# Attention scores of two layers: from plain f32 products to three products of rounded halves and rests

## The chip, the cores and the metric

The kernel runs on one core of one Trainium2 chip. The metric is the device time in microseconds (us) of one execution. TensorE (PE in the profile) multiplies, VectorE (DVE) and ScalarE (ACT) work element by element, GpSimd (POOL) prepares the weights, SyncE (SP) issues the weight loads.

## The reference, cut to what matters

A first block (attention, convolution, memory attention, a feed-forward net) is followed by two equal layers, `hybrid_layer`. The change touches the attention of these two. With 512 tokens, 8 heads of 64 and h = rmsnorm(x):

```
q_a, k_a, v_a, f_a, q_b, kv_b, g_b, gate_a, gate_b = split(h @ w_in)
# fox: 8 heads, causal, with a forget bias c
s = q_a . k_a * 64**-0.5 + c_i - c_j ; p = softmax(s) ; o_a = p @ v_a
# nsa: 8 query heads over 2 key heads, three branches
q   = partial_rope(q_b) ; ks, kw = partial_rope(ks), partial_rope(kw)
kc  = partial_rope(compress_blocks(kc))          # 31 compressed keys
s_c = q . kc * scale   (keys that end before i)  -> o_c
s_s = q . ks * scale   (chosen blocks: all 8)    -> o_s
s_w = q . kw * scale   (window of 512: all)      -> o_w
o_n = g0 * o_c + g1 * o_s + g2 * o_w
x   = x + (sigmoid(gate_a) * (o_a @ w_o_fox) + sigmoid(gate_b) * (o_n @ w_o_nsa)) @ w_out
```

All arrays are float32. With 512 tokens the chosen blocks are all blocks and the window reaches all keys, so both branches are plain causal attention.

## The kernel before, in words

**Matmuls in two precisions.** Every projection is one "tile": 128 output features by 512 tokens, eight chunks of 128 input features, each multiplied three times (lines 497 to 499): weights and activations are each split into a rounded half (`_hi`, type f32r) and a rest (`_lo`), and hi·hi, hi·lo and lo·hi are summed in PSUM. These are f32r matmuls. POOL splits each 128x1024 weight block (lines 442 and 445). The scores of the attention, lines 622 and 776, use the plain f32 type instead.

**The input phase of a layer** (layer 0: about 635 to 778 us, layer 1: about 1418 to 1562 us) runs through 27 jobs, `jobs = ph["in"]`: `gate, kz0, cmp0, kz1, cmp1, kz2, kz3`, then four times a `w1` (half-blocks of the compression weights) with four tiles: `qr0..qr3`, `kr0, kr1, v4, v5`, `v0..v3`, `cp0..cp3`. `kz` are the keys `ka` and `cp` the queries `qa` of fox; `qr` and `kr` are queries and keys of nsa, which need the rotary step. All engines walk the same list with an own loop; PE multiplies job i and then does `finish(i - 1)`; DVE and ACT do in step i what belongs to job i, i-1 or i-2. Each engine takes its instructions in the order of the program and waits at semaphores.

**The rotary step** of a tile i: ACT copies the tile out of PSUM as `rope_hi` (1262), DVE makes `rope_lo` (1711), PE multiplies both by a permutation into the one bank `ps[5]` (592 and 593, in `finish(i)`, which runs after tile i+1), and DVE in its step i+2 forms cosine part `t1` (1698), sine part (1700) and their sum `qb` or `ksw` (1703, 1705), with which it raises `roped`. The next rotation needs `ps[5]` free:

```
def rotate_split(n, slot):
    pe.wait_ge(roped, n - len(ROPE))
    nc.tensor.matmul(ps[5][:, :], rot_r[:, :], rope_hi[:, slot, :], start=True, stop=False)
```

**Attention.** A unit is one head by one block t of 128 queries; its scores are 128x(128(t+1)). Units go in groups of four: two heads, which lie in rows 0 to 63 and 64 to 127 of q and k, for blocks 0 and 3 or blocks 1 and 2. So a group has a pair of units of 128 and a pair of 512 columns, or of 256 and 384. A layer has 8 groups of fox and 16 of nsa. `scores` computes q·k (622; for fox a bf16 product with the forget bias goes first, 608), DVE adds the mask and takes the minimum (1435), ACT exponentiates (1053), DVE scales (1446), PE transposes (632), ACT copies back (1065), PE multiplies with the values (669, 672). In the nsa part a `gate` tile is multiplied in each group step. In the fox part four compressed scores (773 and 776) of 62 columns for four pairs of heads are done, into bank 3. The fox scores start while the last tile, `cp3`, is half done; bank order decides which unit needs which tile taken from PSUM: in layer 0 unit 2 uses the bank of `cp3`, in layer 1 bank 3, that of the compressed scores, held `cp3`.

Of the kernel before, what the change touches and what calls it, by code (L numbers as in the profile page):

```python
# [68 lines left out]
def build(nc, xT, memT, positions, wstream, params, fconst, bconst, lncount, trig2, out):  # L69
# [4 lines left out]
    with ctx:  # L74
# [69 lines left out]
        cmp_t = at("cmp_t", [2, S], f32, R + 66 * KIB)  # L144
        cmp_g = at("cmp_g", [2, 16, 64], f32, R + 70 * KIB)
# [3 lines left out]
        rot_r = at("rot_r", [P], f32r, R + 64 * KIB)  # L149
# [6 lines left out]
        yn_hi = at("yn_hi", [4, S], f32r, R + 52 * KIB)  # L156
        yn_lo = at("yn_lo", [4, S], f32r, R + 60 * KIB)
# [21 lines left out]
        bc = at("bc", [5 * P + 4 * 248 + 8 * P], bf16, Q)  # L179
        Q += (5 * P + 4 * 248 + 8 * P) * 2  # L180
# [33 lines left out]
        rope_split, rot_rounded = sem("rope_split"), sem("rot_rounded")  # L214
        rs_kept, rs_applied, rope_in, gated = sem("rs_kept"), sem("rs_applied"), sem("rope_in"), sem("gated")
# [32 lines left out]
                 "gg": "act", "add": "dve", "fg": "dve", "fu": "dve", "cp": "dve", "kz": "act",  # L248
# [229 lines left out]
        def _(pe):  # L478
# [116 lines left out]
            def scores(i, u0, freed, n=2):  # L595
# [13 lines left out]
                for u in range(i, i + n):  # L609
# [3 lines left out]
                    if kind == "b1":  # L613
                        q_, k_ = q1[r, h // 2, t * P:(t + 1) * P], k1[r, h // 2, :]
                    elif kind == "mem":
                        q_, k_ = qm[r, h // 2, t * P:(t + 1) * P], km[r, h // 2, :]
                    elif kind == "fox":
                        q_, k_ = qa[r, h // 2, t * P:(t + 1) * P], ka[r, h // 2, 0:w]
                    else:
                        q_ = qb[r, h % 4, t * P:(t + 1) * P]  # L620
                        k_ = ksw[r, 0 if kind == "sel" else 1, 0:w]
                    mm = nc.tensor.matmul(s_bank(u)[:, 0:w], q_, k_, start=kind != "fox", stop=True)  # L622
                    mm.then_inc(scored, 1)
# [142 lines left out]
            def compressed_scores(u0, t):  # L766
# [6 lines left out]
                nc.tensor.matmul(ps[3][:, 0:8 * NCMP], identb, cmask[:, t, :], start=True, stop=False)  # L773
                for pair in range(4):
                    both = ps[3][:, 0:8 * NCMP].rearrange("p (g s n) -> p g s n", g=2, s=4)[:, :, pair, :]
                    mm = nc.tensor.matmul(both, qb[:, pair, t * P:(t + 1) * P], kc[:, :, :], start=False, stop=pair == 3)
# [214 lines left out]
        def _(act):  # L991
# [83 lines left out]
            def attend(u0, un, gate_tiles):  # L1075
                for g in range(9):
# [31 lines left out]
            def compressed_exp(u0, t):  # L1108
# [4 lines left out]
                A(cprob[:, :, 0:NCMP], crow[:, 0:8 * NCMP].rearrange("p (h n) -> p h n", h=8), ACT.Exp,  # L1113
# [123 lines left out]
            for l in range(LAYERS):  # L1237
# [4 lines left out]
                for i in range(len(jobs) + 1):  # L1242
                    if i < len(jobs):
                        t = jobs[i]
                        kind, idx, _, _, bank = tiles[t][:5]
                        if kind in ("qr", "kr"):
                            act.wait_ge(blocks_done, filled(t))
                        elif kind not in ("cp", "w1"):
# [740 lines left out]
```

## Time and profile before

| | |
|---|---|
| median of 3 runs | 2212.59 us (2212.02 to 2216.07) |
| span of the profiled execution | 2210.5 us |
| busy PE / PEld / DVE / ACT / POOL | 99% / 78% / 53% / 28% / 68% |
| instructions | 29691 |
| HBM read | 191.85 MB, 88 GB/s over the span |

The profile gives the profiled execution's span only; the median of the runs is 2.1 us above it. PE is the matmul part of TensorE, PEld its loads of the stationary operand, which run beside the matmuls. A record's length holds the way through the array too, so the pace of matmuls is read from start to start. A f32 matmul leaves two PE records (two passes), an f32r matmul one.

### The profile page before, as it was taken

How to read it: one execution, taken by the hardware profiler on the slowest of the kernel's cores; microseconds unless marked ns; L12 is line 12 of the kernel's file. 1: busy time of each engine (PE TensorE's matmuls, PEld its weight loads, DVE VectorE, ACT ScalarE, POOL GpSimd, SP SyncE). 2: the span in 40 equal slices, each digit the busy share in tenths (PEclk: the TensorE clock that was granted, in tenths of full speed). 3: DMA queues.
4: the chain of work that ended last, by engine and by line, in shares of the span. 5: the costliest groups of instructions: out<-in, count | busy, mean ns of one | idle time of the engine just before them, and what ended most of it. 6: DMA issues, size and time to landing. Idle time of an engine off the chain costs nothing.

```text
span 2210.5 us, 29691 instructions
## 1 busy us (share of the span) xinstructions
PE 2184.6 (99%) x10906; PEld 1731.1 (78%) x10907; DVE 1176.8 (53%) x1950; ACT 608.8 (28%) x1439; POOL 1495.6 (68%) x679
## 2 busy tenths in 40 slices
PE   9999999999999999999999999999999999999998
PEld 6876788888887767778888888877677788888886
DVE  8769667774455285557640243562755477411422
ACT  5238322221011165531220121111555412200210
POOL 7660687778876614449887888766334398887884
PEclk9999999999999999999999999999999999999999
DMA  5320233333333312113333333333111132333332
GB/s 194 113 77 1 69 96 101 97 96 102 107 95 126 115 29 58 49 58 101 90 104 97 95 95 96 95 115 115 58 48 49 58 95 86 105 95 95 96 100 71
DMA packets 54921, 195.81 MB, mean 89 GB/s; under 512 B 7313, under 2 KB 7313, under 8 KB 54545
## 3 DMA queue, kind: packets, MB, share of 16 engines
q1 hardware_dynamic: 52496, 187.85, 28.3%
q10 hardware_dynamic: 2304, 6.26, 0.8%
q8 instruction: 88, 1.44, 0.3%
q14 instruction: 33, 0.26, 0.0%
HBM read 191.85 MB, written 2.10 MB: 88 GB/s over the span
## 4 chain that ended last, share of the span: by engine, by line
PE 92%; DVE 5%; ACT 1%; issue 1%; DMA 0%; POOL 0%; SPq 0%; DVEq 0%
PE bank L497 26%; PE bank L499 26%; PE bank L498 26%; PE bank L622 3%; PE bank L632 3%; PE bank L669 1%; DVE t L1333 1%; PE bank L651 1%; PE bank L672 1%; DVE prow L1446 1%; PE bank L510 1%; PE bank L579 1%; DVE bank L1435 1%; ACT prow L1053 1%; DMA w_raw<-wstream 0%
## 5 line engine op out<-in xcount | busy, mean ns | idle before, releaser
L442 POOL TENSOR_TENSOR w_hi<-w_raw,zero 128x1024 fp32r<-128x1024 f32 x336 | 651.5, 1939 | 662.9 <-PE bank L499 651.9
L445 POOL TENSOR_TENSOR w_lo<-w_raw,w_hi 128x1024 fp32r<-128x1024 f32 x336 | 845.2, 2515 | 26.4
L497 PE MATMUL bank<-hn_hi,w_hi 128*128 128x512 f32 x1632 | 646.8, 396 | 3.9 <-POOL w_lo L445 2.6
L499 PE MATMUL bank<-hn_hi,w_lo 128*128 128x512 f32 x1632 | 636.5, 390 | 0.0
L498 PE MATMUL bank<-hn_lo,w_hi 128*128 128x512 f32 x1632 | 636.1, 390 | 0.0
L497 PEld LDWEIGHTS bank<-hn_hi,w_hi 128*128 128x128 f32 x1632 | 306.9, 188 | 73.6 <-issue 5.2
L499 PEld LDWEIGHTS bank<-hn_hi,w_lo 128*128 128x128 f32 x1632 | 306.6, 188 | 65.4
L498 PEld LDWEIGHTS bank<-hn_lo,w_hi 128*128 128x128 f32 x1632 | 307.0, 188 | 62.5 <-issue 1.4
L497 PE MATMUL bank<-hid_hi,w_hi 128*128 128x512 f32 x688 | 267.7, 389 | 0.0
L499 PE MATMUL bank<-hid_hi,w_lo 128*128 128x512 f32 x688 | 267.6, 389 | 0.0
L498 PE MATMUL bank<-hid_lo,w_hi 128*128 128x512 f32 x688 | 267.6, 389 | 0.0
L1506 DVE TENSOR_TENSOR x<-bank,x 128x512 f32<-128x512 f32 x64 | 44.2, 691 | 372.8 <-PE bank L499 372.8
L1306 ACT ACTIVATE sq<-tmp 128x512 f32<-128x512 f32 x64 | 40.4, 632 | 431.4 <-DVE tmp L1824 431.4
L499 PEld LDWEIGHTS bank<-hid_hi,w_lo 128*128 128x128 f32 x688 | 129.1, 188 | 27.0
L498 PEld LDWEIGHTS bank<-hid_lo,w_hi 128*128 128x128 f32 x688 | 129.2, 188 | 26.9
L497 PEld LDWEIGHTS bank<-hid_hi,w_hi 128*128 128x128 f32 x688 | 129.1, 188 | 26.6
L1824 DVE SCALAR_TENSOR_TENSOR tmp<-bank,rs 128x512 f32<-128x512 f32 x64 | 44.1, 692 | 185.0 <-PE bank L499 185.0
L1065 ACT ACTIVATE pT<-bank 128x256 f32<-128x256 f32 (+2 forms) x240 | 98.1, 453 | 140.4 <-PE bank L632 139.6
L1828 DVE TENSOR_TENSOR hid_lo<-sq,hid_hi 128x512 fp32r<-128x512 f32 x64 | 123.2, 1929 | 1.5 <-ACT hid_hi L1308 1.5
L1435 DVE CUSTOM_DVE_ANT_0 bank<-bank,bc 128x128 f32<-128x128 f32 (+1 forms) x192 | 89.5, 520 | 63.5 <-PE bank L622 63.5
L632 PEld LDWEIGHTS bank<-fc,prow 128*128 128x128 f32 x640 | 68.4, 141 | 57.3 <-issue 29.9
L1039 ACT ACTIVATE hn_hi<-x,par 128x512 fp32r<-128x512 f32 x40 | 29.0, 724 | 273.3 <-DVE x L1506 273.3
(304 smaller groups left out, 2646.9 us busy)
## 6 DMA issues: line engine op xcount, KB each, us to landing
w_raw<-wstream SPq DMA_DIRECT2D x352, 512.0 KB, 3.6
x<-xT SPq DMA_DIRECT2D x4, 512.0 KB, 7.6
out<-yout ACTq DMA_DIRECT2D x8, 256.0 KB, 2.2
mem_x<-memT SPq DMA_DIRECT2D x1, 1024.0 KB, 12.2
lnc<-lncount ACTq DMA_DIRECT2D x1, 1024.0 KB, 5.9
cs<-trig ACTq DMA_DIRECT2D x2, 512.0 KB, 4.4
par<-params ACTq DMA_DIRECT2D x1, 696.0 KB, 5.2
bc<-bconst ACTq DMA_DIRECT2D x1, 664.0 KB, 7.1
```

Source lines behind the costliest of these rows:

```text
L442: nc.gpsimd.tensor_tensor(w_hi[:, slot, :], w_raw[:, slot, :], zeros, ALU.add).then_inc(w_rounded, 1)
L445: nc.gpsimd.tensor_tensor(w_lo[:, slot, :], w_raw[:, slot, :], w_hi[:, slot, :].bitcast(f32), ALU.subtract).then_inc(w_split, 1)
L497: nc.tensor.matmul(ps[bank][:, 0:cols_], wh, a_h, start=c == 0, stop=False)
L498: nc.tensor.matmul(ps[bank][:, 0:cols_], wh, a_l, start=False, stop=False)
L499: mm = nc.tensor.matmul(ps[bank][:, 0:cols_], wl, a_h, start=False, stop=c == chunks - 1)
L622: mm = nc.tensor.matmul(s_bank(u)[:, 0:w], q_, k_, start=kind != "fox", stop=True)
L632: mm = nc.tensor.transpose(ps[4 + u % 2][:, c * P:(c + 1) * P], prow[:, u % 4, c * P:(c + 1) * P], ident)
L1065: A(turned(u)[:, u % 4, 0:width(u)], ps[4 + u % 2][:, 0:width(u)], ACT.Copy).then_inc(p_kept, 1)
L1435: V.tensor_tensor_reduce(out=s_bank(u)[:, 0:w], in0=s_bank(u)[:, 0:w], in1=causal[:, S - w:S], scale=1.0, scalar=3e38, op0=ALU.add, op1=AL ...
L1506: V.tensor_tensor(x[:, m, :], ps[tiles[t][4]][:, :], x[:, m, :], ALU.add).then_inc(dve_took, 1)
L1824: V.scalar_tensor_tensor(out=tmp[:, n % 3, :], in0=ps[tiles[up[i]][4]][:, :], scalar=0.0, in1=rs[:, :], op0=ALU.max, op1=ALU.mult).then_in ...
L1828: V.tensor_tensor(hid_lo[:, i - 1, :], sq[:, (n - 1) % 2, :], hid_hi[:, i - 1, :].bitcast(f32), ALU.subtract).then_inc(ff_lo, 1)
```

## The change

It replaces each f32 product q·k of fox and nsa by three f32r products, q_hi·k_hi, q_hi·k_lo, q_lo·k_hi, summed in PSUM; the two units of a pair alternate. The compressed scores are done likewise, on 32 instead of 31 columns per key head (the mask covers the 32nd). For that, `qa`, `ka`, `qb`, `ksw` and `kc` become pairs `_hi` and `_lo`: ACT writes `_hi`, DVE subtracts it from the value in PSUM to get `_lo`. The rotated sum stays in `ps[5]` until both are taken. The buffers are laid out anew (`qb_lo` 54, `ksw_lo` 64, `qa_hi` 68, `qa_lo` 76 KiB into the region; `yn_hi` and `yn_lo` now lie where `qb` does; `lf`, `fgs`, `z32`, `s8`, `rot_r`, `cmp_t`, `cmp_g` moved). ACT does the exponentials of the first two fox rows before it takes `cp3`.

```diff
@@ scores(): after the bias products of fox
-                    elif kind == "fox":
-                        q_, k_ = qa[r, h // 2, t * P:(t + 1) * P], ka[r, h // 2, 0:w]
...
-                    mm = nc.tensor.matmul(s_bank(u)[:, 0:w], q_, k_, start=kind != "fox", stop=True)
-                    mm.then_inc(scored, 1)
+                for i2 in range(i, i + n, 2):
+                    for part in range(3):
+                        for u in (i2, i2 + 1):
...
+                            if kind == "fox":
+                                q_, k_ = (qa_hi, qa_hi, qa_lo)[part], (ka_hi, ka_lo, ka_hi)[part]
...
+                            mm = nc.tensor.matmul(s_bank(u)[:, 0:w], q_, k_, start=kind != "fox" and part == 0,
+                                                  stop=part == 2)
@@ compressed_scores()
-                    mm = nc.tensor.matmul(both, qb[:, pair, t * P:(t + 1) * P], kc[:, :, :], start=False, stop=pair == 3)
+                    for part in range(3):
+                        q_, k_ = (qb_hi, qb_hi, qb_lo)[part], (kc_hi, kc_lo, kc_hi)[part]
+                        mm = nc.tensor.matmul(both, q_[:, pair, t * P:(t + 1) * P], k_[:, :, :], start=False,
+                                              stop=pair == 3 and part == 2)
@@ ACT, input phase, step i
+                    if 0 <= i - 2 < len(jobs) and tiles[jobs[i - 2]][0] in ("qr", "kr"):
...
+                        act.wait_ge(rope_full, 6 * l + idx_of_rope(jobs[i - 2]) + 1)
+                        A((qb_hi if kind == "qr" else ksw_hi)[:, idx, :], ps[5][:, :], ACT.Copy).then_inc(rope_rounded, 1)
...
+                        elif kind == "cp":
+                            if i == len(jobs) - 1:
+                                exp_row(FIRST["fox", l])
+                                exp_row(FIRST["fox", l] + 1)
+                            act.wait_ge(cp_scaled, 4 * l + idx + 1)
+                            A(qa_hi[:, idx, :], src[:, :], ACT.Copy).then_inc(cp_rounded, 1)
@@ DVE, input phase, step i: (a) rotary of job i-2, (b) rope_lo or scale of job i, then
-                            V.tensor_tensor(qb[:, idx, :], ps[5][:, :], t1[:, :], ALU.add).then_inc(roped, 1)
+                        V.tensor_tensor(ps[5][:, :], ps[5][:, :], t1[:, :], ALU.add).then_inc(rope_full, 1)
...
+                    if 0 <= i - 2 < len(jobs) and tiles[jobs[i - 2]][0] in ("qr", "kr"):
...
+                        dve.wait_ge(rope_rounded, 6 * l + idx_of_rope(jobs[i - 2]) + 1)
+                        V.tensor_tensor(lo[:, idx, :], ps[5][:, :], hi[:, idx, :].bitcast(f32),
+                                        ALU.subtract).then_inc(roped, 1)
+                    if 0 <= i - 1 < len(jobs) and tiles[jobs[i - 1]][0] in ("kz", "cp"):
...
+                        V.tensor_tensor(lo[:, idx, :], ps[bank][:, :], hi[:, idx, :].bitcast(f32),
+                                        ALU.subtract).then_inc(dve_took, 1)
```

DVE in the input phase of layer 0, around the tiles `qr1` to `qr3`, before (`cs` is the sine and cosine table, `t` is `t1`):

```order
L1711 SCALAR_TENSOR_TENSOR rope_lo<-bank,rope_hi 128x512 [waits rope_in]
L1698 SCALAR_TENSOR_TENSOR t_124<-bank,cs_110 128x512 [waits roped,rotated,trig_scaled,fg_parts]
L1700 TENSOR_TENSOR bank<-bank,cs_110 128x512
L1703 TENSOR_TENSOR qb<-bank,t_124 128x512 [waits dve_took,dve_chain]
L1711 SCALAR_TENSOR_TENSOR rope_lo<-bank,rope_hi 128x512 [waits rope_in]
L1698 SCALAR_TENSOR_TENSOR t_124<-bank,cs_110 128x512 [waits roped,rotated,trig_scaled,fg_parts]
```

and the same place of the changed kernel:

```order
L1744 SCALAR_TENSOR_TENSOR rope_lo<-bank,rope_hi 128x512 [waits rope_in]
L1735 SCALAR_TENSOR_TENSOR t_130<-bank,cs_116 128x512 [waits roped,rotated,trig_scaled,fg_parts]
L1737 TENSOR_TENSOR bank<-bank,cs_116 128x512
L1739 TENSOR_TENSOR bank<-bank,t_130 128x512 [waits dve_took,dve_chain]
L1744 SCALAR_TENSOR_TENSOR rope_lo<-bank,rope_hi 128x512 [waits rope_in]
L1754 TENSOR_TENSOR qb_lo<-bank,qb_hi 128x512 [waits rope_rounded]
L1735 SCALAR_TENSOR_TENSOR t_130<-bank,cs_116 128x512 [waits roped,rotated,trig_scaled,fg_parts]
```

What frees `ps[5]` (and raises `roped`) was the fourth row; now it is the sixth, and the `rope_lo` of a tile two jobs later stands ahead of it.

DVE a few tiles on, around job `v4`, where `scale` (L1349 before, L1386 now) multiplies the new tile by the norm factor; before:

```order
L1698 SCALAR_TENSOR_TENSOR t_124<-bank,cs_110 128x512 [waits roped,rotated,trig_scaled,fg_parts]
L1700 TENSOR_TENSOR bank<-bank,cs_110 128x512
L1705 TENSOR_TENSOR ksw<-bank,t_124 128x512 [waits dve_took,dve_chain]
L1349 TENSOR_TENSOR bank<-bank,rs 128x512 [waits blocks_done]
L1698 SCALAR_TENSOR_TENSOR t_124<-bank,cs_110 128x512 [waits roped,rotated,trig_scaled,fg_parts]
```

and now:

```order
L1735 SCALAR_TENSOR_TENSOR t_130<-bank,cs_116 128x512 [waits roped,rotated,trig_scaled,fg_parts]
L1737 TENSOR_TENSOR bank<-bank,cs_116 128x512
L1739 TENSOR_TENSOR bank<-bank,t_130 128x512 [waits dve_took,dve_chain]
L1386 TENSOR_TENSOR bank<-bank,rs 128x512 [waits blocks_done]
L1754 TENSOR_TENSOR ksw_lo<-bank,ksw_hi 128x512 [waits rope_rounded]
L1735 SCALAR_TENSOR_TENSOR t_130<-bank,cs_116 128x512 [waits roped,rotated,trig_scaled,fg_parts]
```

Here the scaling of `v4` stands ahead of the subtraction that frees `ps[5]`.

PE in the fox part of layer 0, the scores of a pair with 384 columns; before (L622 is one instruction for each unit, with two passes; the numbers are the banks):

```order
L608 MATMUL bank0<-c3_96,bc_133 128x384
L608 MATMUL bank1<-c3_96,bc_133 128x384
L622 MATMUL bank0<-ka_87,qa_86 128x384
L622 MATMUL bank1<-ka_87,qa_86 128x384
L632 MATMUL bank4<-fc_132,prow_126 128x128 x4
```

and now (the bias products, L616, and the pair of 256 columns stand ahead of it):

```order
L642 MATMUL bank0<-ka_hi_87,qa_hi_88 128x384
L642 MATMUL bank1<-ka_hi_87,qa_hi_88 128x384
L642 MATMUL bank0<-ka_lo_86,qa_hi_88 128x384
L642 MATMUL bank1<-ka_lo_86,qa_hi_88 128x384
L642 MATMUL bank0<-ka_hi_87,qa_lo_89 128x384
L642 MATMUL bank1<-ka_hi_87,qa_lo_89 128x384
```

Two instructions with four passes became six with one pass each.

## Rows read from the trace of the kernel before

**Rows 1.** The page: busy us (share of the span) xinstructions, by engine
```profile
PE 2184.6 (99%) x10906; PEld 1731.1 (78%) x10907; DVE 1176.8 (53%) x1950; ACT 608.8 (28%) x1439; POOL 1495.6 (68%) x679
```
**Rows 2.** Waits, whole span: engine tile <- released by: us, times, longest
```profile
POOL w_hi L442 <- PE bank L499: 651.9, 273, 73.3
```
**Rows 3.** Busy in stretches (fox, nsa of layer 0): us, engines (x), PEclk, DMA share, GB/s
```profile
779.00:821.00 42.00, 39.25 (x306) 25.30 (x308) 37.85 (x143) 28.83 (x97) 3.76 (x2) 1.00 0.09 26
821.00:970.00 149.00, 149.00 (x900) 109.30 (x901) 84.84 (x256) 83.08 (x269) 63.81 (x30) 1.00 0.18 54
```
**Rows 4.** Timeline, PE, two groups of nsa: start, us, engine, line, what
```profile
868.68 1.35 PE L622 MATMUL bank<-ksw,qb 64*128 64x128 f32 x8
869.96 1.09 PE L632 MATMUL bank<-fc,prow 128*128 128x128 f32 x8
...
878.06 1.35 PE L622 MATMUL bank<-ksw,qb 64*128 64x256 f32 x8
879.34 1.09 PE L632 MATMUL bank<-fc,prow 128*128 128x128 f32 x8
```
**Rows 5.** Timeline, PE, a pair of 512 columns and compressed scores, layer 0
```profile
779.76 1.13 PE L622 MATMUL bank<-ka,qa 64*128 64x512 f32 x4
780.82 0.28 PE L773 MATMUL bank<-bc 128*128 128x248 bf16 x1
780.94 1.00 PE L776 MATMUL bank<-kc,qb 128*128 128x62 f32 x8
781.78 0.38 PE L608 MATMUL bank<-c,bc 96*128 96x256 bf16 x2
```
**Rows 6.** Timeline, PE, f32r matmuls of 256 columns in the first block
```profile
79.19 0.28 PE L497 MATMUL bank<-mn_hi,w_hi 128*128 128x256 f32 x1
79.31 0.28 PE L498 MATMUL bank<-mn_lo,w_hi 128*128 128x256 f32 x1
```
**Rows 7.** Timeline of all engines, rotary steps of layer 0
```profile
691.22 0.39 PE L592 MATMUL bank<-rope_hi,rot_r 128*128 128x512 f32 x1
691.42 0.60 ACT L1262 ACTIVATE rope_hi<-bank 128x512 fp32r<-128x512 f32 x1 [6.58 <-PE bank L499]
691.45 0.39 PE L593 MATMUL bank<-rope_lo,rot_r 128*128 128x512 f32 x1
692.05 0.69 DVE L1711 SCALAR_TENSOR_TENSOR rope_lo<-bank,rope_hi 128x512 fp32r<-128x512 f32 x1 [2.79 <-ACT rope_hi L1262]
692.66 0.68 DVE L1698 SCALAR_TENSOR_TENSOR t<-bank,cs 128x512 f32<-128x512 f32 x1
...
697.11 0.39 PE L592 MATMUL bank<-rope_hi,rot_r 128*128 128x512 f32 x1
...
701.57 0.39 PE L592 MATMUL bank<-rope_hi,rot_r 128*128 128x512 f32 x1
...
703.65 0.69 DVE L1703 TENSOR_TENSOR qb<-bank,t 128x512 f32<-128x512 f32 x1
```
**Rows 8.** Timeline, the rotation after tile v4, layer 0
```profile
717.85 0.39 PE L592 MATMUL bank<-rope_hi,rot_r 128*128 128x512 f32 x1
...
718.05 0.70 DVE L1349 TENSOR_TENSOR bank<-bank,rs 128x512 f32<-128x512 f32 x1 [3.86 <-PE bank L499]
```
**Rows 9.** Timeline, after the last tile cp3: layer 0, then layer 1
```profile
778.48 0.69 DVE L1729 SCALAR_TENSOR_TENSOR qa<-bank,rs 128x512 f32<-128x512 f32 x1 [0.39 <-PE bank L499]
779.23 0.61 PE L608 MATMUL bank<-c,bc 96*128 96x512 bf16 x2 [0.57 <-DVE qa L1729]
...
1562.39 0.69 DVE L1729 SCALAR_TENSOR_TENSOR qa<-bank,rs 128x512 f32<-128x512 f32 x1 [0.47 <-PE bank L499]
...
1564.00 0.28 PE L773 MATMUL bank<-bc 128*128 128x248 bf16 x1
```
**Rows 10.** The longest idle time of PE: timeline, and the stretch behind it
```profile
9.19 0.50 PE L497 MATMUL bank<-hn_hi,w_hi 128*128 128x512 f32 x1 [2.62 <-POOL w_lo L445]
...
12.00:20.00 8.00, 7.89 (x30) 6.05 (x29) 7.33 (x12) 6.86 (x13) 7.12 (x4) 0.87 1.01 407
```

More of the change, by code:

```diff
@@ L148, in build @@
         rope_lo = at("rope_lo", [2, S], f32r, R + 20 * KIB)
-        rot_r = at("rot_r", [P], f32r, R + 64 * KIB)
+        rot_r = at("rot_r", [P], f32r, R + 80 * KIB + 512)
         cs2 = at("cs2", [2, S], f32, R + 82 * KIB)
@@ L1241, in _ @@
                 jobs = ph["in"]
-                for i in range(len(jobs) + 1):
+                for i in range(len(jobs) + 2):
+                    if 0 <= i - 2 < len(jobs) and tiles[jobs[i - 2]][0] in ("qr", "kr"):
+                        kind, idx = tiles[jobs[i - 2]][:2]
+                        act.wait_ge(rope_full, 6 * l + idx_of_rope(jobs[i - 2]) + 1)
+                        A((qb_hi if kind == "qr" else ksw_hi)[:, idx, :], ps[5][:, :], ACT.Copy).then_inc(rope_rounded, 1)
                     if i < len(jobs):
@@ L1247, in _ @@
                             act.wait_ge(blocks_done, filled(t))
+                            if kind == "qr" and idx == 0:
+                                act.wait_ge(cmp_full, 2 * (l + 1))
                         elif kind not in ("cp", "w1"):
@@ L1270, in _ @@
                             ins.then_inc(act_took, 1)
-                    if i >= 1:
+                    if 1 <= i <= len(jobs):
                         t = jobs[i - 1]
@@ L1792, in _ @@
                             rows = slice(64 * g, 64 * g + 64)
-                            ins = V.tensor_tensor(kc[rows, g, :], tmp[rows, 0, sl], tmp[rows, 1, sl], ALU.add)
-                        ins.then_inc(cmp_kept, 1)
-                link(V.memset(cprob[:, :, NCMP:32], 0.0))
+                            link(V.tensor_tensor(kc[rows, g, 0:NCMP], tmp[rows, 0, sl], tmp[rows, 1, sl], ALU.add))
+                        link(V.tensor_copy(kc_hi[:, :, :], kc[:, :, :]))
+                        V.tensor_tensor(kc_lo[:, :, :], kc[:, :, :], kc_hi[:, :, :].bitcast(f32),
+                                        ALU.subtract).then_inc(cmp_kept, 1)
                 attend(FIRST["fox", l], FIRST["nsa", l], ph["gates"])
@@ L1949, in _constants @@
     q = np.arange(S).reshape(TT, P).T
-    cmask = np.where(end[None, None, None, :] <= q[:, :, None, None], f(0), f(BIG))
-    cmask = np.broadcast_to(cmask, (P, TT, 8, NCMP)).reshape(P, -1)
+    last = np.append(end, S)
+    cmask = np.where(last[None, None, None, :] <= q[:, :, None, None], f(0), f(BIG))
+    cmask = np.broadcast_to(cmask, (P, TT, 8, 32)).reshape(P, -1)
     sel = np.zeros((P, 8, P), f)
```

102 lines of the change are left out of this document (62 added, 40 removed).

## The prediction

> **What bounds the kernel now.** I read the page first: PE is busy for 2184.6 of 2210.5 us [rows 1]. Then who waits: POOL, which prepares the weights, waits 651.9 us for PE to free a block [rows 2], so neither weights nor DMA hold PE back. Then the stretches that the change touches. In the nsa part PE is busy for all of its 149 us; in the fox part for 39.25 of 42 us, with DVE at 37.85 beside it, so there the two share the bound [rows 3]. Hence the rule of the whole sum: a microsecond added to or taken from PE's stream counts in full, except in fox, and so does each moment in which PE, which takes matmuls in order, stands before a semaphore. The last point is seen in the trace: after cp3 PE stood idle 0.57 us until DVE had taken the tile [rows 9].
>
> **The scores, per pass.** A pair of 512 columns takes from 779.76 to 780.82, 1.06 us, for four records: both row halves run at once, so that is two passes. f32r matmuls of 512 columns start 0.23 us apart (691.22, 691.45) [rows 7]. A nsa group takes 1.28 us in both kinds (868.68 to 869.96, 878.06 to 879.34) [rows 4, 5]. The group of blocks 0 and 3 is a pair of 128 and a pair of 512 columns: 1.28 - 1.06 = 0.22 us for the two passes of 128 columns, 0.11 each. A pass in proportion to its columns is then 0.43 for 512, 0.215 for 256 and 0.325 for 384, and 1.06 - 2 x 0.43 = 0.20 us is left for the load ahead and the drain behind, which the switch between 128 and 64 rows lays bare once in each group.
>
> Now three f32r passes each. 512 columns: 0.23. 256 columns: 0.12 (79.19, 79.31) [rows 6]. 384: 0.175, midway. 128 columns have no row; what bounds them from below is the load of the stationary operand, which eight records of 62 columns show at 0.84/8 = 0.105 us, and I take 0.11 [rows 5]. From above: as two f32 passes, 0.22; I come to that as a rival. The kind (0, 3) goes from 2 x 0.11 + 2 x 0.43 = 1.08 to 3 x 0.11 + 3 x 0.23 = 1.02: 0.06 less. The kind (1, 2) goes from 2 x 0.215 + 2 x 0.325 = 1.08 to 3 x 0.12 + 3 x 0.175 = 0.885: 0.195 less. All this assumes that f32r pairs on 64 rows run at once as the f32 pairs do.
>
> The Trainium skill, in "TensorE: Matmul & The Clock Gate", section "LDWEIGHTS (loading the stationary operand)", says that this load takes a time set by the columns, at 1.2 per ns, whatever the rows: 107 ns. The row agrees with it (105 ns), and it speaks against this change, because a half-height operand is loaded three times where two loads were: by the page's figure the narrow pair would go from 0.22 to an estimated 0.32 us and win nothing.
>
> **nsa**: 16 groups in a layer, 8 of each kind: 8 x 0.255 = 2.04 us less; two layers: **-4.1**, in full, because PE is the bound there.
>
> **fox**: 8 groups: 4 x 0.255 = 1.0 us less in a layer. The compressed scores go from 8 records to 12 of 64 columns, at 0.11 us each: 0.44 more, four times: 1.75 more. If PE alone counted, +0.75 in a layer; DVE's share hides some. The ends are -1.0 (all added PE time hidden) and +1.75; I take +0.35, two layers: **+0.7**. DVE's own work here grows by 8 columns in a few instructions, nothing.
>
> **The rotary steps.** This is the largest term. `ps[5]`, which the next rotation overwrites, was free after the sum (L1703). Now it stays taken until ACT has copied it and DVE has subtracted, and DVE's subtraction stands behind `rope_lo` of the tile two jobs later. That in turn waits for ACT's copy of a tile that PE has only just finished. But PE's next instruction, right behind that same tile, is the rotation that needs `ps[5]`. So what was long done becomes a wait that can't be shorter than this chain, read from the tile qr2 [rows 7]: PE reaches the rotation at 691.22; ACT copies from 691.42 to 692.02; DVE makes `rope_lo` from 692.05; its next instruction starts 0.61 later, at 692.66, and would be the subtraction: 0.69, to 693.35 (sources in PSUM and SBUF as for L1703). PE reacts 0.06 later, as after cp3 (778.48 + 0.69 to 779.23) [rows 9], and then loads with nothing to overlap, half of the 0.20 above: 693.5. That is 2.3 us instead of none. The copy of the rotated tile by ACT itself is hidden, since the rotation before it is 5.9 us old.
>
> Which rotations: that of qr1 (behind qr2), and that of qr2 (behind qr3). The one of qr3 comes after half a w1 and half a tile, 4.46 us after qr2's (697.11, 701.57). Its chain has no new tile in it: rotation to end of sum 703.65 + 0.69 - 701.57 = 2.77, ACT 0.05 + 0.60, DVE 0.03 + 0.69, PE 0.06: 4.20. It fits with 0.26 to spare; nothing lost, 0.3 if I am wrong. kr0's waits for qr3's `ps[5]`, whose subtraction runs during kr1: nothing. kr1's (behind v4) waits for kr0's subtraction, which stands behind the scaling of v4: 718.05 + 0.61 + 0.69 + 0.06 + 0.10 = 719.5 against 717.85 [rows 8]: 1.65. The others are not followed by a rotation. A layer: 2 x 2.3 + 1.65 = 6.25, two layers **+12.5**. Ends: each link could be 0.1 shorter or longer: 11 to 14.
>
> **The start of fox.** cp3 is now scaled in PSUM, copied by ACT, subtracted by DVE. From the start of the scaling: 0.69 + 0.05 + 0.60 + 0.03 + 0.69 + 0.06 = 2.12. Layer 0, unit 2 needs the bank: 778.48 + 2.12 = 780.6 instead of 779.23: 1.4. Layer 1, only the compressed scores do: 1562.39 + 2.12 = 1564.5 instead of 1564.0: 0.5 [rows 9]. Together **+1.9**. The moved exponentials were done long before.
>
> **At nothing**: the other copies and subtractions, 4 kz, 3 cp and the narrow ones of `kc` in a layer. DVE is busy for 53% and ACT for 28% [rows 1], and those banks are used again two or more tiles (5.4 us each) later; each would cost its 0.7 us if that cover were gone. The new layout of buffers moves no instruction and I find no new wait in it. POOL and SP have the same instructions.
>
> **Sum**: -4.1 + 0.7 + 12.5 + 1.9 = +11.0 us on the span of 2210.5: 2221.5. The median of the runs lies 2.1 above the span, so 2223.6.
>
> **Rivals.**
> 1. *Narrow f32r matmuls are no faster than f32 ones.* Against it: 256 columns run at 0.12 [rows 6]; for it: no row below 256. A product of 128 then costs 0.22 instead of 0.11 in 24 pairs of 128 (12 in a layer), 24 x 0.33 = +7.9, and 96 compressed products 0.1 more each, +9.6, part of both hidden in fox. About +12: 2236.
> 2. *f32r pairs don't run on the two row halves at once.* For it: no row shows such a pair. Against it: f32 pairs and the 64-column products do. Each group's passes double: +1.02 and +0.885 in 48 groups = +46, less what fox hides: 2262.
> 3. *The stalls let the clock fall.* PE's longest idle time now is 2.62 us, at the start, and the stretch behind it had a granted clock of 0.87 [rows 10], which is a mix of the two levels, 1.2 and 2.4 GHz. It cost 8 x 0.13 = 1.0 us or more. Four stalls of 2.3 us at 1.0 to 1.7 each: +4 to +7: 2229. Against it: each new stall has more than 5 us of dense matmuls on both sides, and the start had little ahead of it.
> 4. *The other side: PE isn't held at the rotation.* If the next tile's matmuls, whose bank and weights are ready, went past the waiting rotation, the 12.5 would vanish: -4.1 + 0.7 + 1.9 = -1.5: 2211.1, not slower. It decides from the point where 11 of the 12.5 are hidden. Against it: at 779.23 PE stood idle for 0.57 us, and the next gate tile or transposes behind it did not go ahead [rows 9].
>
> **How the numbers follow.** Forecast 0.68, rival 1 0.08, rival 2 0.06, rival 3 0.12, rival 4 0.06. The forecast's own range, from the ends of its terms (scores -3 to -5, fox -1 to +2, rotary 11 to 14, start 1 to 2.5), is 2219 to 2228. The range for 8 in 10 goes from there up over rival 3 and nearly to rival 1: 2217 to 2234. A measurement of this kernel can tell 0.2%, 4.4 us, from no change. Rival 4 is "within", with some of its own spread below -0.2%, and a little of the forecast's lower tail falls within: slower 0.88, same 0.08, faster 0.04.
>
> **What would show it.** In the trace after: idle time of PE before `rope_hi` x `rot_r` (L600) of 2.2 us for qr1 and qr2 and 1.5 for kr1, in both layers, released by DVE's subtraction (L1754), none for qr0, qr3 and kr0; score groups of nsa of about 1.2 and 1.1 us instead of 1.28; f32r records of 64 rows starting in pairs some ns apart; twelve compressed records in 1.3 us; granted clock 1.00 throughout. Idle time before L600 below 1 us refutes the largest term; score groups above 1.3 us refute the second.

## The result, and the profile after

The changed kernel takes 2233.16 us (median of 4 runs, 2230.57 to 2234.36), the kernel before 2212.60 (4 runs beside it, 2212.02 to 2216.07): a ratio of 1.0088, 95% interval 1.0077 to 1.01, so 20.6 us slower. 2223.6 was forecast, with a range to 2234: the sign and the range hold, the most likely value was 9.6 us too low. The profiled run is the slowest of the four, 2234.36 us; its span is 2232.6 against 2210.5, so 22.1 us are to be explained.

The page after, beside [rows 1]: PE has 224 more matmuls (four in each of the 48 groups of pairs, four in each of the eight compressed products) and 9.2 us more busy time, less than half of the 22.1.

```profile
PE 2193.8 (98%) x11130; PEld 1749.8 (78%) x11131; DVE 1195.5 (54%) x1980; ACT 622.1 (28%) x1459; POOL 1495.4 (67%) x679
```

To find the place, I took the start of the same instruction in both traces and subtracted: the offset. The step is what the offset grew by since the row above (ahead of the first row it is +0.4, that of qr0's rotation, 685.15 before and 685.58 after). "Clock at 0.5" counts the stretches with a granted clock of 0.5 since the row above, called falls from here on; those at the start and the end of the kernel are left out.

```
start (us) of                     before    after   offset   step   clock at 0.5
rotation qr1, layer 0             691.22   693.91    +2.70   +2.3
rotation qr2, layer 0             697.11   703.78    +6.67   +4.0    1 (694.5)
rotation qr3, layer 0             701.57   709.89    +8.33   +1.7    1 (704.7)
rotation kr1, layer 0             717.85   727.82    +9.97   +1.6
first fox bias, layer 0           774.78   784.86   +10.07   +0.1
first compressed scores, layer 0  780.82   792.12   +11.30   +1.2
first nsa scores, layer 0         820.84   834.71   +13.87   +2.6    1 (800.3)
first tile of the mix, layer 0   1020.73  1032.74   +12.01   -1.9
rotation kr1, layer 1            1501.77  1523.38   +21.61   +9.6    2 (1489.8, 1500.0)
first compressed scores, layer 1 1564.00  1586.23   +22.23   +0.6
first nsa scores, layer 1        1604.02  1628.01   +23.99   +1.8    1 (1588.8)
first tile of the mix, layer 1   1803.92  1826.04   +22.11   -1.9
```

The largest term of the prediction, the rotary steps, is where it was put. PE's waits in layer 0 from the rotary steps to fox (engine, tile and line it waited in, releaser: us, times, longest):

```profile
PE bank L600 <- DVE qb_lo L1754: 4.2, 2, 2.1
PE bank L616 <- DVE qa_lo L1761: 1.9, 1, 1.9
PE bank L600 <- DVE ksw_lo L1754: 1.5, 1, 1.5
```

And the chain at qr1's rotation, from the timeline of all engines (start, us, engine, line, what, idle time ahead):

```profile
691.42 0.39 PE L507 MATMUL bank<-hn_hi,w_lo 128*128 128x512 f32 x1
691.85 0.60 ACT L1299 ACTIVATE rope_hi<-bank 128x512 fp32r<-128x512 f32 x1 [1.52 <-PE bank L507]
...
692.48 0.69 DVE L1744 SCALAR_TENSOR_TENSOR rope_lo<-bank,rope_hi 128x512 fp32r<-128x512 f32 x1 [2.78 <-ACT rope_hi L1299]
693.09 0.68 DVE L1754 TENSOR_TENSOR qb_lo<-bank,qb_hi 128x512 fp32r<-128x512 f32 x1
...
693.91 0.47 PE L600 MATMUL bank<-rope_hi,rot_r 128*128 128x512 f32 x1 [2.10 <-DVE qb_lo L1754]
...
703.78 0.47 PE L600 MATMUL bank<-rope_hi,rot_r 128*128 128x512 f32 x1 [2.10 <-DVE qb_lo L1754]
...
727.82 0.47 PE L600 MATMUL bank<-rope_hi,rot_r 128*128 128x512 f32 x1 [1.47 <-DVE ksw_lo L1754]
```

PE ends the tile, ACT copies, DVE makes rope_lo, DVE subtracts and only then releases ps[5]. In [rows 7] and [rows 8] the same rotations stood without idle time. What the forecast did not have is in the next view, the stretches around these waits (us, busy of PE, PEld, DVE, ACT, POOL, granted clock, DMA share, GB/s):

```profile
691.40:694.50 3.10, 1.00 (x5) 0.53 (x4) 1.29 (x2) 0.60 (x1) 2.53 (x2) 1.00 0.27 107
694.50:697.90 3.40, 3.40 (x10) 2.63 (x9) 2.00 (x3) 0.60 (x1) 1.74 (x1) 0.50 0.01 2
697.90:704.70 6.80, 4.70 (x23) 3.30 (x23) 1.37 (x3) 0.60 (x1) 2.79 (x2) 1.00 0.00 0
704.70:708.10 3.40, 3.40 (x13) 2.09 (x10) 2.61 (x4) 0.60 (x1) 1.47 (x1) 0.50 0.23 46
```

Right behind each wait of 2.1 us the granted clock is 0.50, the lower of the two levels (1.2 GHz), and PE does 10 and 13 matmuls in a time in which it does 15 at full clock. That happens at all four waits of 2.1 us, and once more in each layer's fox part:

```profile
796.80:800.30 3.50, 2.27 (x18) 1.50 (x20) 3.28 (x15) 2.89 (x10) 0.00 (x0) 1.00 0.01 2
800.30:803.70 3.40, 3.40 (x18) 2.21 (x16) 2.74 (x12) 2.36 (x8) 0.00 (x0) 0.50 0.00 0
```

The scores. Timeline of PE, one nsa group of each kind, to be held against [rows 4]:

```profile
882.03 0.33 PE L642 MATMUL bank<-ksw_hi,qb_hi 64*128 64x128 f32 x2
882.19 0.28 PE L642 MATMUL bank<-ksw_lo,qb_hi 64*128 64x128 f32 x2
882.30 0.28 PE L642 MATMUL bank<-ksw_hi,qb_lo 64*128 64x128 f32 x2
882.42 0.45 PE L642 MATMUL bank<-ksw_hi,qb_hi 64*128 64x512 f32 x2
882.70 0.40 PE L642 MATMUL bank<-ksw_lo,qb_hi 64*128 64x512 f32 x2
882.93 0.41 PE L642 MATMUL bank<-ksw_hi,qb_lo 64*128 64x512 f32 x2
883.26 0.98 PE L654 MATMUL bank<-fc,prow 128*128 128x128 f32 x7
...
891.38 0.39 PE L642 MATMUL bank<-ksw_hi,qb_hi 64*128 64x256 f32 x2
...
892.45 1.09 PE L654 MATMUL bank<-fc,prow 128*128 128x128 f32 x8
```

Each row is a pair (x2) on the two row halves, and the next pass starts 0.11 us later at 128 columns and 0.23 at 512, behind the first pass of each 0.05 more: pairs run at once, and narrow f32r matmuls are fast. The groups take 1.23 (forecast 1.22) and 1.07 us (forecast 1.085). The start of fox in layer 0 and the compressed scores, against [rows 9] and [rows 5]:

```profile
790.69 0.60 PE L616 MATMUL bank<-c,bc 96*128 96x512 bf16 x2 [1.93 <-DVE qa_lo L1761]
791.23 0.49 PE L642 MATMUL bank<-ka_hi,qa_hi 64*128 64x512 f32 x2
...
792.16 0.28 PE L800 MATMUL bank<-kc_hi,qb_hi 128*128 128x64 f32 x1
792.27 0.28 PE L800 MATMUL bank<-kc_lo,qb_hi 128*128 128x64 f32 x1
...
793.39 0.28 PE L800 MATMUL bank<-kc_hi,qb_lo 128*128 128x64 f32 x1
793.51 0.40 PE L616 MATMUL bank<-c,bc 96*128 96x256 bf16 x2
```

Twelve records in 1.35 us, 0.11 each, where eight took 0.84.

### The profile page after: what moved, and what is told of

Same layout as the page of the kernel before. It is cut to its first block, busy times and chain, and to the rows that moved or that the text cites. A ratio compares the mean times of both kernels' runs of the same rounds, so it can differ in the third digit from the quotient of the medians.

```text
span 2232.6 us, 30187 instructions
## 1 busy us (share of the span) xinstructions
PE 2193.8 (98%) x11130; PEld 1749.8 (78%) x11131; DVE 1195.5 (54%) x1980; ACT 622.1 (28%) x1459; POOL 1495.4 (67%) x679
## 4 chain that ended last, share of the span: by engine, by line
PE 91%; DVE 5%; issue 1%; ACT 1%; DMA 0%; POOL 0%; SPq 0%; DVEq 0%
PE bank L505 26%; PE bank L507 26%; PE bank L506 26%; PE bank L654 3%; PE bank L642 2%; PE bank L691 1%; DVE t L1370 1%; PE bank L627 1%; PE bank L673 1%; PE bank L518 1%; PE bank L694 1%; DVE prow L1483 1%; PE bank L587 1%; DVE bank L1472 0%; PE bank L800 0%
```

## The experiments

Ten kernels were measured, in four runs each where no number is given; the kernel before took 2212.7 to 2213.0 (medians) beside them. One run of each was profiled, and what is said of waits and of falls is read from that one. "Offset" is, as above, against the trace of before.

**e1: the subtraction first.** In DVE's step the block at L1754 stands ahead of rope_lo:

```diff
+                    if 0 <= i - 2 < len(jobs) and tiles[jobs[i - 2]][0] in ("qr", "kr"):
+                        ...
+                        V.tensor_tensor(lo[:, idx, :], ps[5][:, :], hi[:, idx, :].bitcast(f32),
+                                        ALU.subtract).then_inc(roped, 1)
                     if i < len(jobs) and tiles[jobs[i]][0] in ("qr", "kr"):
                         ... rope_lo ...
                     if i < len(jobs) and jobs[i] in SCALED:
                         scale(jobs[i])
-                    (the same block)
```

> The changed kernel with one block moved: in DVE's step the subtraction that frees ps[5] stands ahead of rope_lo and of the scaling of the tile two jobs later. Theory A (the rotation of qr1, qr2 and kr1 waits because the subtraction stands behind rope_lo, and the clock falls because of that wait): PE's idle time before rope_hi x rot_r goes from 2.1, 2.1 and 1.5 us to none in both layers, 12.3 us less, and the four stretches with a granted clock of 0.5 behind qr1's and qr2's rotations go with them, 4 x 1.7 = 6.8 us less: 2233.2 - 12.3 - 6.8 = about 2214. Rival B (the clock falls there because of the work in the rotary steps, not of the wait): only the stalls go, about 2221. Rival C (the wait is really for ACT's copy or for rope_lo itself, whatever the order): 2233.

Measured: 2217.10 us (10 runs, 2215.86 to 2219.01). The rotations of qr1 and qr2 have the offset of the kernel's start, +0.3; 0.5 us more come before qr3's, with a wait of 0.35, and stay (L1744 is the moved subtraction, L1751 rope_lo):

```profile
690.24 0.69 DVE L1744 TENSOR_TENSOR qb_lo<-bank,qb_hi 128x512 fp32r<-128x512 f32 x1 [0.67 <-ACT qb_hi L1271]
...
691.53 0.39 PE L600 MATMUL bank<-rope_hi,rot_r 128*128 128x512 f32 x1
...
692.36 0.69 DVE L1751 SCALAR_TENSOR_TENSOR rope_lo<-bank,rope_hi 128x512 fp32r<-128x512 f32 x1 [1.43 <-ACT rope_hi L1299]
```

The subtraction now runs 1.3 us before PE gets to the rotation, under a tile's matmuls. All four falls in the rotary steps are gone too. A instead of B and C: 16 of the 20.6 us go with one moved block. It is 3 us above A's 2214, with its ratio at 1.0018 (1.0009 to 1.0028). Against A, the profiled execution has 0.5 us more before qr3's rotation in each layer, and the wait of 1.9 us for cp3's bank was followed by a longer fall than those that A left in place, 781.8 to 792.0. Layer 0's rotary steps, then that fall:

```profile
691.00:715.00 24.00, 23.65 (x110) 17.99 (x109) 12.44 (x19) 5.82 (x9) 16.39 (x8) 1.00 0.30 102
```

```profile
781.80:792.00 10.20, 10.20 (x46) 7.01 (x45) 5.87 (x21) 3.85 (x13) 2.00 (x1) 0.50 0.18 53
```

**e4: the kernel before, with the order alone changed.** The sum `V.tensor_tensor(qb, ps[5], t1)` (L1703) moved behind rope_lo and the scaling, and ACT's wait before `rope_hi` put on `rotated` instead of `roped`, as in the changed kernel; nothing is split, and all scores are plain f32.

> The kernel before with nothing but the order changed: DVE's sum that frees ps[5] stands behind rope_lo and the scaling of the tile two jobs later, as in the changed kernel; scores and everything else are plain f32 as before. Theory A (the order alone makes the stalls, the stalls make the clock fall): 2 x 6.2 = 12.3 us of stalls and four stretches at clock 0.5 for 6.8 us: 2212.6 + 19.1 = about 2231.7. Rival B (order gives the stalls but the fall of the clock needs the f32r copies or scores too): about 2225. Rival C (the stalls come from ACT's added copy in the chain rather than from the order): 2212.6, no change.

Measured: 2232.08 us (2229.03 to 2235.63), the time of the changed kernel and A's 2231.7. Its timeline:

```profile
692.45 0.69 DVE L1705 SCALAR_TENSOR_TENSOR rope_lo<-bank,rope_hi 128x512 fp32r<-128x512 f32 x1 [3.58 <-ACT rope_hi L1262]
693.06 0.68 DVE L1716 TENSOR_TENSOR qb<-bank,t 128x512 f32<-128x512 f32 x1
...
693.89 0.47 PE L592 MATMUL bank<-rope_hi,rot_r 128*128 128x512 f32 x1 [2.17 <-DVE qb L1716]
```

The same wait, 2.17 us, with no copy of the rotated tile by ACT. So the order makes the stall, and C falls, and B with it: the clock falls without the f32r copies and scores of the change. The profiled execution, the fastest (2229.03), has two of the four falls (703.0 and 1494.9): behind the same wait of 2.2 us the clock sometimes stays up. The four times, 2229.03, 2230.70, 2233.45 and 2235.63, go with mean clocks of 0.997, 0.997, 0.995 and 0.994.

**e2 and e8: PE kept busy in the wait.** Both leave every semaphore as it is and put bf16 matmuls into a spare bank ahead of the rotation:

```diff
                     if kind in ("qr", "kr"):
                         pe.wait_ge(rot_rounded, l + 1)
+                        if t in (jobs[9], jobs[10], jobs[14]):        # qr1, qr2, kr1
+                            stay_awake(9 if t != jobs[14] else 6)     # e8: 4, and none at kr1
```

> The changed kernel with bf16 matmuls of 512 columns into the spare bank put on PE just ahead of the rotations that wait (9 each ahead of qr1's and qr2's, 6 ahead of kr1's), so that PE works where it stood idle for 2.1 or 1.5 us; the wait for DVE's subtraction stays. Theory A (idle PE lets the clock fall): the rotations start as late as before, but the four stretches at clock 0.5 behind them go: 4 x 1.7 = 6.8 us less than the changed kernel's 2233.2, about 2226.5. Rival B (the falls have another cause than the idle PE): the falls stay, 2233. Rival D (the added matmuls last longer than the idle time): up to 2 us more than either, shown by no idle time left ahead of the rotation.

> The changed kernel with 4 instead of 9 bf16 matmuls of 512 columns put on PE ahead of the rotations of qr1 and qr2, and none ahead of kr1's: 0.9 of 2.1 us is filled and about 1.2 us of idle time is left. The stalls stay as long. Theory A (the clock falls behind a long idle time, and 1.2 us is not enough): the four stretches at 0.5 go in most executions, mean clock 0.996 to 0.997, about 2226.4 to 2229. Rival B (any idle time of over a microsecond amid dense work does it): the falls stay, clock 0.994 to 0.995, about 2232 to 2234.

Measured: e2 2229.01 us (2228.56 to 2230.76), e8 2229.03 (2228.19 to 2230.64). The rotations come as late as in the changed kernel (6.3 to 6.4 us have come together by kr1's rotation, in both kernels and layers), but no fall lies behind them. First e2, then e8, layer 0, where 1.23 us of idle time was left; for each, the timeline (it has eight of the nine matmuls of e2) and then the stretch:

```profile
691.99 1.89 PE L565 MATMUL bank<-bc 128*128 128x512 bf16 x8
694.03 0.47 PE L600 MATMUL bank<-rope_hi,rot_r 128*128 128x512 f32 x1
```

```profile
691.00:715.00 24.00, 23.64 (x107) 16.72 (x107) 10.55 (x16) 3.56 (x6) 12.85 (x6) 1.00 0.24 85
```

```profile
691.34 1.04 PE L565 MATMUL bank<-bc 128*128 128x512 bf16 x4
693.60 0.47 PE L600 MATMUL bank<-rope_hi,rot_r 128*128 128x512 f32 x1 [1.23 <-DVE qb_lo L1756]
```

```profile
691.00:706.00 15.00, 12.55 (x58) 8.34 (x57) 7.16 (x11) 2.40 (x4) 8.58 (x4) 1.00 0.13 44
```

So stall and clock are two costs with two cures. From qr1's to qr2's rotation the changed kernel takes 9.87 us and e2 8.26: 1.6 us is what one such fall costs. The medians come down by 4.1 us, not by 6.4. The changed kernel's 2233.2 does not stand for four falls in every run (its fastest took 2230.57), and more of the fox part ran at 0.5 here: in e2 a fall of 10.2 us (788.3 to 798.5), in e8 one of 6.8 (789.4) and one of 3.4, where the changed kernel has two of 3.4. e2 is 2.5 us above A's 2226.5, of which an estimate of 1.7 is that longer fall (3.4 us more at half the clock). In e8 the upper end of A's 2226.4 to 2229 holds, with its mean clocks of 0.996 and 0.997; its rival B falls.

**e3: the scores as one f32 product.** `for part in range(1)` with `q_.bitcast(f32), k_.bitcast(f32)`, in all three kinds of score.

> The changed kernel with each of the three-part scores (fox, nsa, compressed) as one f32 product of the two rounded halves; it leaves out the two products with the rests. All that ACT and DVE produce, all waits and the order are those of the changed kernel. It gives the price of the products alone. nsa: groups go back to 1.28 us, 2 x 1.74 = 3.5 us more. fox: compressed scores 12 records of 0.11 become 8, 1.75 less in all, pairs 2.0 more, partly hidden by DVE. Theory A (the clock falls in fox, at 800.3 and 1588.8, because the f32r scores give PE less work between its waits): both falls go, 3.4 us less: 2233.2 + 3.5 + 0.3 - 3.4 = about 2233.5. Rival B (they fall because of the idle time ahead of cp3's bank and cmask): they stay, about 2237. In both the stalls of the rotary steps and the four falls there stay.

Measured: 2234.23 us (2231.62 to 2236.82). The nsa part is back to before's length to 0.03 us, the stalls and the four falls stay, there is none in fox, and one more behind kr1's wait of 1.5 us (1523.8). So A rather than B, but on one profiled execution, and the four times, 2231.6 to 2236.8, reach from one to the other. In fox the three parts cost what is missing here: from the first compressed scores to the first nsa scores layer 0 takes 39.95 us, 40.02 in the kernel before, 42.59 in the changed one with one fall in it.

**e5: the banks too.** e1, and the cp tiles on banks 0 to 3 in both layers, with `first = (0, 1, 2, 7)` as the order of the score banks, so that unit 2 needs cp2's bank.

> The kernel of e1 (subtraction ahead of rope_lo) and the q tiles cp0 to cp3 on banks 0 to 3 in both layers, so that unit 2 of fox in layer 0 needs cp2's bank and no longer cp3's; only the compressed scores still wait for cp3, as in layer 1. In e1's trace PE stood idle for 1.9 us ahead of unit 2 in layer 0, and a stretch of 10.2 us with a granted clock of 0.5 lay there; from the start of fox to the first nsa score layer 0 lost 6.0 us and layer 1 1.55 us. Theory A (the wait for cp3's bank costs 1.2 us and is also what lets the clock fall): layer 0 becomes like layer 1, 4.4 less than e1's 2217.1: about 2212.7. Rival B (the clock falls in fox because three short f32r passes leave PE less work, wait or not): only 1 us less, about 2216, with a stretch at 0.5 still in layer 0's fox part.

Measured: 2213.33 us (10 runs, 2212.08 to 2215.71), ratio 1.000 (0.9991 to 1.0009): the changed computation at the time of the kernel before. The wait before unit 2 is gone, 0.57 us before the compressed scores is left. The ten times lie in three groups, near 2212.3, 2213.8 and 2215.6; the profiled one of the last group has a fall in each fox part (789.4 and 1574.4). The five fastest, 2212.08 to 2212.87, are A's 2212.7, and B is half right: falls in fox don't need cp3's wait. The fall in layer 0:

```profile
789.40:792.80 3.40, 3.40 (x18) 2.45 (x16) 2.89 (x12) 1.49 (x6) 0.00 (x0) 0.50 0.00 0
```

**e6 and e7: split from SBUF.** e6 leaves DVE's order and writes the sum to t1, so that ps[5] is free at once; e7 scales the cp tiles into `tmp` as well.

```diff
-                        V.tensor_tensor(ps[5][:, :], ps[5][:, :], t1[:, :], ALU.add).then_inc(rope_full, 1)
+                        V.tensor_tensor(t1[:, :], ps[5][:, :], t1[:, :], ALU.add).then_inc(rope_full, 1)
             def rotate_split(n, slot):
-                pe.wait_ge(roped, n - len(ROPE))
+                pe.wait_ge(rope_full, n - len(ROPE))
```

> The changed kernel, DVE's order as it is there, but the rotated sum is written to t1 in SBUF instead of back to ps[5]; ACT copies and DVE subtracts from t1, and PE's next rotation waits for the sum alone (rope_full). Theory A (the stalls come from ps[5] being held until the subtraction): PE's idle time before all six rotations of a layer is gone, the 0.5 before qr3's that e1 still had too, and no stretch at 0.5 behind them: 2233.2 - 12.3 - 6.8 = 2214.1, up to 2 more for a longer fall in fox as in e1. Rival B (the order of DVE's instructions delays rope_lo or the sum itself so that PE waits all the same): above 2217. ACT's copy and the subtraction may take another time from SBUF than from PSUM; nothing waits for them.

> The kernel of e6, and the scaled q tiles (cp) are written to tmp in SBUF as well, so that their banks are free from the scaling on as in the kernel before; ACT and DVE split them from there, and the fox scores wait for the finished pair of tiles by a semaphore. Theory A (all waits of the change were for PSUM held through the split): no idle time of PE beyond that of before in the rotary steps (12.3 us less than the changed kernel) and at the start of fox (1.2 and 0.5 less), none of the six stretches at 0.5. What is left of the change is nsa -1.74 in each layer, fox +0.9 to +1.0 in each, the start of the kernel +0.3: 2212.6 - 3.5 + 2.0 + 0.3 = about 2211.4, 0.05% less than before. Rival B (the clock falls in fox without the waits too, from its lighter f32r work): 1.7 to 5 us more, 2213 to 2216.

Measured: e6 2216.69 us (10 runs, 2213.95 to 2217.71), e7 2215.95 (11 runs, 2213.16 to 2220.03; ratio 1.0012, 1.0003 to 1.0021). The stalls of 2.1 and 1.5 us are gone in both, so A's cause holds (e6 is 0.6 us above A's upper end), but e7 misses A's 2211.4 and is no faster than e5. Its rival B, falls in fox without the waits, has the number (2213 to 2216), and e7's profile has such a fall at 789.6, e6's one at 1570.2. Two more things were priced wrong. Before qr3's rotation 0.51 us of waiting stays in each layer. It is now for the sum, which starts late because the subtraction ahead of it takes longer from SBUF. The subtractions of e7 by source (min/median/max ns), and those of one of them beside POOL:

```profile
L1762 DVE TENSOR_TENSOR qb_lo<-t,qb_hi x8: 692/1021/1318, 693.2 to 1493.5; 128x512 fp32r<-128x512 f32 x8
L1762 DVE TENSOR_TENSOR ksw_lo<-t,ksw_hi x4: 1878/1912/1947, 720.0 to 1512.3; 128x512 fp32r<-128x512 f32 x4
...
L1769 DVE TENSOR_TENSOR qa_lo<-tmp,qa_hi x8: 1058/1129/1167, 761.5 to 1566.7; 128x512 fp32r<-128x512 f32 x8
```

```profile
719.48 1.90 POOL L450 TENSOR_TENSOR w_hi<-w_raw,zero 128x1024 fp32r<-128x1024 f32 x1 [3.21 <-PE bank L507]
720.04 1.88 DVE L1762 TENSOR_TENSOR ksw_lo<-t,ksw_hi 128x512 fp32r<-128x512 f32 x1
...
721.45 2.73 POOL L453 TENSOR_TENSOR w_lo<-w_raw,w_hi 128x1024 fp32r<-128x1024 f32 x1
```

From PSUM the same subtraction took 0.69 us in all twelve cases of e1. The second: the fox part of layer 1 stays 1.73 us longer than before's although cp3's wait of 0.54 is gone, where e1 had 1.55 with it. So taking the wait away gained nothing there, and what counts is the scores' own work.

**e9 and e10: which scores cost it in fox.** e5, with the compressed scores alone as one f32 product of the rounded q, and with the fox pairs alone so.

> The kernel of e5 (no rotary stalls but 0.5 before qr3, no wait for cp3's bank before unit 2) with the compressed scores alone as one f32 product of the rounded q with the f32 key, 8 records instead of 12; it leaves out the products with the rest of q. It asks how much of fox's surplus the four added records of each of the four compressed products of a layer are. e5 takes 2212.2 in its executions without a fall of the clock, and a layer's fox part 45.32 + 1.55 in e1's layer 1. Theory A (the records count in full: 4 x 4 x 0.11 = 1.8 a layer): 2212.2 - 3.6 = 2208.6 at the lowest, median about 2209.5. Rival B (DVE and ACT set the end in fox, the records are hidden): no less than 2211.5. Between the two, each in part: 2210.

> The kernel of e5 with the fox pairs alone as one f32 product of the rounded halves; it leaves out their products with the rests. The compressed and nsa scores keep three parts. By the passes (1.0 us a layer saved by the three short f32r passes) PE has 2 x 1.0 us more to do in fox. Theory A (fox is bound by PE): 2212.2 + 2.0 = 2214.2 in executions without a fall of the clock. Rival B (fox is bound by DVE, pairs are hidden): 2212.2 or up to 0.5 less. On the clock: if the lighter three-part pairs are what lets it fall in fox, as e3's profile without a fall there suggests, all executions stay at 0.999 and the times lie within 1 us of each other, where e5's lay in three groups 1.7 apart; if not, the three groups stay.

Measured: e9 2209.58 us (10 runs, 2209.01 to 2211.20; ratio 0.9988, 0.9978 to 0.9997), e10 2212.96 (10 runs, 2212.68 to 2213.55). The fox part of layer 1 (first bias to first nsa scores) of before, e1, e9 and e10, one row each, none with a fall in it (e1 stands for e5, whose profile has a fall there; in this layer both have the same waits):

```profile
1558.70:1604.02 45.32, 42.78 (x325) 28.05 (x325) 40.04 (x150) 29.63 (x101) 7.11 (x4) 1.00 0.11 34
```

```profile
1564.31:1611.18 46.87, 43.83 (x373) 31.66 (x373) 40.46 (x150) 30.43 (x102) 7.04 (x4) 1.00 0.11 34
```

```profile
1557.48:1602.81 45.33, 42.11 (x357) 29.91 (x356) 40.51 (x150) 30.27 (x102) 7.09 (x4) 1.00 0.11 35
```

```profile
1559.56:1606.72 47.16, 44.48 (x342) 29.82 (x341) 40.96 (x150) 30.38 (x102) 7.19 (x4) 1.00 0.11 33
```

With eight compressed records instead of twelve the part is as long as before: of the four products' four added records each, 1.8 us at 0.11, 46.87 - 45.33 = 1.54 lie on the path (e9, A; its median is the 2209.5 that A gave). The pairs do the opposite: their three short passes leave PE 0.65 us less to do (44.48 - 43.83), of which 0.29 reach the end (47.16 - 46.87), between e10's A and B. On the clock: e10's ten times lie within 0.9 us, where e5's lay over 3.6. Over all twelve profiles, the four kernels with f32 pairs in fox (before, e3, e4, e10) have no fall in either layer's fox part; of the eight with three-part pairs, seven have at least one, and e9 none, though four of its ten times stand apart from the other six, 1 us above them. That points to the lighter pairs as what lets it fall there, and e3, which has the waits of the changed kernel, speaks against the waits as its cause. Five of the ten falls in fox begin 1.7 to 2.4 us behind a wait of PE of 1.2 us before a transpose, but six more such waits have none behind them. It isn't settled: the executions of the kernel before, with f32 pairs, lie between 2212.0 and 2216.1, some of them 1.7 or 3.4 us above the rest, and only one of them was profiled.

## Why the prediction was right, and where it was not

By its own terms, us on the span of the profiled executions; "measured" is taken from traces in which no fall lies in that part.

```
term                     forecast  measured  from
rotary stalls              +12.5     +12.7   e2: 6.33 and 6.36 to kr1's rotation
start of fox                +1.9      +1.8   after: 1.23 and 0.54
nsa scores                  -4.1      -3.7   after: -1.86 a layer
fox scores                  +0.7      +2.0   e1, layer 1: +1.00, twice
start of the kernel          0        +0.4   +0.1 to +0.9 from execution to execution
the rest: falls of clock     0        +8.9   6.4 rotary, 2.3 fox; a rival at +4 to +7
sum                        +11.0     +22.1
```

**The rotary steps** were right in place, size and chain: waits before qr1, qr2 and kr1, none before qr0, qr3, kr0, in both layers, and the rotations late by 2.3, 2.4 and 1.65 us (e2) where 2.3, 2.3 and 1.65 were worked out from the rows of before. e1 and e4 show the cause from both sides: the place of one DVE instruction behind another that needs a tile PE has just ended. Rival 4, that PE isn't held, fell.

**The nsa scores** were right by kind, 1.23 and 1.07 us. Rivals 1 and 2 fell with them: pairs of 128 columns pass in 0.11 us and both row halves run at once. The 0.20 us that was put down to one switch in each group came out right as a sum, but lies in three places of the first group's rows: 0.05 behind the first pass of 128, 0.05 behind the first of 512, 0.10 before the transposes.

**The fox scores** failed in one term, "DVE's share hides some". I took +0.35 a layer between ends of -1.0 and +1.75, as if DVE hid a part of what is added; it came to +1.0. e9 shows 1.54 of the added 1.8 on the path, and e10 that the pairs' saving, which I had set at 1.0 in full, brings 0.29 and takes 0.65 from PE's busy time. The row had it: PE is busy for 39.25 of 42 us [rows 3], so most of what is added to PE there must lengthen the part. Even PE alone, +0.75 by my own terms, was nearer than the value I chose.

**The clock** is the step that failed. The prediction had "granted clock 1.00 throughout" among its signs, and against rival 3, the falling clock, it wrote: "Against it: each new stall has more than 5 us of dense matmuls on both sides". With that it gave rival 3, 2229, a chance of 0.12, and it is what happened: 6.4 of the 8.9 us stand behind the four waits of 2.1 us, and e2 and e8 take them away with the stalls left in place. The price of 1.0 to 1.7 us for each holds (1.6), though only its lower end had a row. The one row on it [rows 10], 2.62 us of idle time with 0.87 behind it, was the nearest to a wait of 2.1 us, and it was set aside for a reason that no row bore out. That 0.87 is itself the mean over a fall, from 10.7 us on:

```profile
10.72:14.13 3.41, 3.06 (x8) 2.19 (x8) 3.38 (x6) 3.41 (x7) 1.41 (x1) 0.50 1.04 425
```

On the span, rival 3 stands at +16.5 (11.0 and the middle of 4 to 7) and the measurement at +22.1. Of the 5.6 between them 2.3 are the two falls in fox, of which no rival spoke and whose cause is still open, 1.3 fox's scores, 0.9 the larger price of the four falls, and 1.1 small differences in the other terms.

**The range** held by luck. The forecast's own range ended at 2228; 2233.2 lies inside only because the whole range went on past rival 3, at 2229, toward rival 1, at 2236, which fell.

None of the versions that compute all three parts is faster than the kernel before: e5 equals it at 2213.3. e9's 2209.6 shows what the compressed scores are worth; a plain f32 q for them would need 8 KB a partition while fox runs, and it was not tried.

## What to carry to other kernels

When a value is split in place in PSUM, ask who needs that bank next and what stands ahead of the releasing instruction on its engine: one order of DVE's step cost 12.7 us in stalls and 6.4 in clock, and moving a block took away both but for 1 us. Price a stall of PE of 2 us as 2 plus 1.6 where a row of the profile shows the clock below 1.00 behind idle time; four spare matmuls in the wait kept it up here (e8). In a part like fox here, where PE was busy for 39.25 of 42 us and DVE for 37.85, count what is added to PE nearly in full (1.54 of 1.8) and what is saved at less than half (0.29 of 0.65).

## What the runs showed of the hardware that was not expected

The granted clock went to 0.50 behind idle times of PE of 2.1 us amid dense matmuls: at 4 of 4 in the profiled runs of the changed kernel and of e3, at 2 of 4 in e4. Behind 1.5 us (kr1's) it did once in eight such waits (after, e3, e4, e8), behind 1.2 us (e8, rotary steps) at none of four. Behind the 1.9 us before cp3's bank it did within 1 us in e1 and e2 and within 2.3 us in e8, and it stayed up for at least 9 us in the changed kernel, e3 and e6. The length alone does not decide: at the start of the kernel, around 9 us, idle times of 2.0 to 2.3 us had no fall behind them in five profiles (after, e3, e5, e7, e8), and 2.6 us (before) and 1.8 us (e2) had one. What does is open.

A DVE subtraction of 512 columns took 0.68 to 0.69 us with one operand in PSUM, whatever POOL did. With both in SBUF (e6 and e7) it took 0.69 us while POOL was idle, and 0.78 to 1.95 us where a POOL instruction ran when it began: all 28 of those ended 0.55 us after that POOL instruction, however early they had begun. The one at 720.04 ended at 721.92, POOL's `w_hi` at 721.37. Alone it takes 0.69 us, so it had got little done until then. The Trainium skill has the rule, in "GPSIMD Engine Reference", section "Specifications": GpSimd's way into SBUF is shared with VectorE, and they contend when a DVE instruction has two SBUF inputs. The trace of e7 agrees, with these numbers.
